# Stage boundaries of a two-block transformer kernel rebuilt: tile-wise norms, three products begun together, in-place weight slots, padded keys

## What is computed

```python
def first_block(x, ...):                    # two layers
    for l in range(2):
        u = rmsnorm(x, pre_mix_g[l])
        m = token_mixer(u, ...)              # 8 GQA heads (2 key heads) and 8 latent (MLA) heads, gates, w_o
        x = x + rmsnorm(m, post_mix_g[l])
        h = rmsnorm(x, pre_ffn_g[l]) @ w_ffn_up[l]          # 1024 -> 4096
        f = jnp.square(jax.nn.relu(h)) @ w_ffn_down[l]
        x = x + rmsnorm(f, post_ffn_g[l])
    return x

def second_block(x, ...):                   # layer 0: S5 scan, layer 1: stick-breaking attention
    h = rms_norm(x, norm_mix[0]);  x = x + s5_mixer(h, ...)
    x = x + conv_ffn(rms_norm(x, norm_ffn[0]), ...)          # 1024 -> 2 x 2816 -> 1024
    kv = rms_norm(x, norm_kv) @ kv_w
    h = rms_norm(x, norm_mix[1]);  x = x + stick_breaking_attention(h, w_q, k, v, w_o)
    x = x + conv_ffn(rms_norm(x, norm_ffn[1]), ...)
    return rms_norm(x, norm_final)
```

## Time and profile before

| | us |
|---|---|
| median of the runs | 3228.28 |
| the profiled execution | 3231.55 |
| its span | 3229.8 |
| TensorE matmul busy | 2923.6 (91%), 12788 matmuls |
| VectorE busy | 1589.4 (49%) |
| ScalarE busy | 1147.9 (36%) |
| GpSimd busy | 848.6 (26%) |
| granted TensorE clock, mean | 0.938 |
| weight chunk, from issue to landing, median | 3.4 |
| ScalarE: high half of a 1024-column chunk, of a 768-column chunk | 1.04, 0.84 |
| VectorE: low half of a 1024-column chunk, of a 768-column chunk | 1.23, 0.96 |
| ScalarE per norm tile: copy with gain, square | 0.71, 0.61 |

### The profile page before, as it was taken

One profiled execution on the slowest core, in us unless ns is written; L12 is line 12 of the kernel. 1 busy time (PEld: TensorE's weight loads), 2 busy tenths in 40 slices (PEclk: granted clock), 3 DMA queues, 4 the chain that ended last, 5 costly groups with the idle time before them and its releaser, 6 DMA issues.

```text
span 3229.8 us, 36156 instructions
## 1 busy us (share of the span) xinstructions
PE 2923.6 (91%) x12788; PEld 2341.5 (72%) x12788; DVE 1589.4 (49%) x2048; ACT 1147.9 (36%) x1716; POOL 848.6 (26%) x672
## 2 busy tenths in 40 slices
PE   7898997999979989979998674699999999999998
PEld 5566775888756667758886464578888778878887
DVE  4478434323264873343333767455542447655532
ACT  4355333223244552332223222233321336632322
POOL 2255003304132540132132837112210002212210
PEclk9799998999988999989999766799999998999999
DMA  3100231333220102212332110223333220023232
GB/s 127 33 27 27 87 95 62 97 98 98 92 66 27 33 27 93 96 62 96 98 98 79 52 34 16 69 78 98 98 98 106 89 82 4 27 85 96 94 104 85
DMA packets 75531, 236.91 MB, mean 73 GB/s; under 512 B 9520, under 2 KB 18144, under 8 KB 75360
## 3 DMA queue, kind: packets, MB, share of 16 engines
q1 hardware_dynamic: 74432, 231.43, 22.4%
q0 software_dynamic: 928, 3.21, 0.3%
HBM read 228.31 MB, written 2.10 MB: 71 GB/s over the span
## 4 chain that ended last, share of the span: by engine, by line
PE 62%; issue 22%; POOL 7%; DVE 6%; ACT 2%; SPq 1%; DMA 0%; POOLq 0%; DVEq 0%; ACTq 0%
PE bank L1615 20%; PE bank L1617 19%; PE bank L1616 19%; POOL TMP L732 3%; PE bank L1875 2%; POOL FF L717 1%; POOL FF L724 1%; DVE S5S L1489 1%; PE bank L1783 1%; DVE UL L1248 1%; POOL FF L737 1%; DVE S5M L1432 1%; PE bank L1830 1%; DVE S5S L1480 1%; SPq L665 1%
## 5 line engine op out<-in xcount | busy, mean ns | idle before, releaser
L1238 DVE TENSOR_TENSOR WL<-RAWW,WH 128x1024 fp32r<-128x1024 f32 (+2 forms) x424 | 538.5, 1270 | 1239.4 <-ACT WH L946 1239.0
L1615 PE MATMUL bank<-UH,WH 128*128 128x512 f32 (+1 forms) x1920 | 772.9, 403 | 151.0 <-DVE UL L1248 109.3
L1616 PE MATMUL bank<-UL,WH 128*128 128x512 f32 (+1 forms) x1920 | 761.3, 397 | 0.0
L1617 PE MATMUL bank<-UH,WL 128*128 128x512 f32 (+1 forms) x1920 | 760.3, 396 | 0.0
L946 ACT ACTIVATE WH<-RAWW 128x1024 fp32r<-128x1024 f32 (+2 forms) x424 | 437.7, 1033 | 846.0 <-PE bank L1617 839.1
L1615 PEld LDWEIGHTS bank<-UH,WH 128*128 128x128 f32 (+1 forms) x1920 | 368.3, 192 | 254.7 <-DVE UL L1248 96.8
L1616 PEld LDWEIGHTS bank<-UL,WH 128*128 128x128 f32 (+1 forms) x1920 | 369.4, 192 | 78.2 <-issue 2.5
L1617 PEld LDWEIGHTS bank<-UH,WL 128*128 128x128 f32 (+1 forms) x1920 | 368.4, 192 | 79.2
L698 POOL TENSOR_TENSOR SQUARES<-SQUARES,TMP 128x512 f32<-128x512 f32 x56 | 78.2, 1397 | 556.5 <-ACT TMP L966 554.8
L1615 PE MATMUL bank<-HH,WH 128*128 128x512 f32 x512 | 199.2, 389 | 0.0
L1616 PE MATMUL bank<-HL,WH 128*128 128x512 f32 x512 | 199.2, 389 | 0.0
(11 more groups left out here) (316 smaller groups left out, 4801.3 us busy)
## 6 DMA issues: line engine op xcount, KB each, us to landing
RAWW<-weights SPq DMA_DIRECT2D x424, 512.0 KB, 3.4
X<-x SPq DMA_DIRECT2D x8, 256.0 KB, 4.8
FF<-tables POOLq DMA_DIRECT2D x2, 1024.0 KB, 6.5
U<-S5U SPq DMA_DIRECT2D x16, 128.0 KB, 2.4
GEL<-U SPq DMA_DIRECT2D x128, 16.0 KB, 1.8
out<-FF SPq DMA_DIRECT2D x8, 256.0 KB, 2.5
S5B<-s_b POOLq DMA_DIRECT2D x1, 512.0 KB, 3.9
S5C<-s_c POOLq DMA_DIRECT2D x1, 512.0 KB, 4.5
```

The lines of the kernel that those rows point to most:

```text
L1238: dve.tensor_tensor(slot_words(WL, c % CUT, size), slot_words(RAWW, c % RAW, size), f32(slot_words(WH, c % CUT, size)), ALU.subtract).then ...
L1615: nc.tensor.matmul(out_, w[0], x_[0], start=start, stop=False, **how)
L1616: nc.tensor.matmul(out_, w[0], x_[1], start=False, stop=False, **how)
L1617: return nc.tensor.matmul(out_, w[1], x_[0], start=False, stop=stop, **how)
```

## The change

`SLOTS = 4`, `LEAD = 3` and `LINEAR_BANKS = (0, 1, 4, 5)` replace `RAW` and `CUT`. `WL` lies on top of `RAWW`: VectorE writes the low half over the raw chunk, both halves have four slots, and SyncE loads a slot when its product is through. Cuts are steps of their own. A linear run behind a norm issues its first three products k-tile by k-tile, side by side in three banks, then a tree of sums on VectorE over the eight squares (now in FF), then the fourth product, then one ones-matmul for the factor; evacuations catch up by two per product. The next norm's work follows each finished tile of X. VectorE scales all eight post-norm tiles. The keys of the two key heads lie in separate tiles, padded with zeros to 128 rows. The layer loop is written out twice. Constants come on ScalarE's queue, X and the first weights in turn on SyncE's.

```diff
+    def product(x):
+        ring = LEAD + 1 if norm and x >= 2 else 2
...
+        mm[x].bank = LINEAR_BANKS[mm[x].j % (LEAD + 1)] if norm else mm[x].j % 2
+    if norm:
+        for x in range(LEAD):
+            product(x)
+        for step in mm:
+            step.lead = mm[:]
+        if early:
+            early()
+        plan.add("tree", norm=norm)
+    for x in range(len(mm), len(jobs) + 1):
         if x < len(jobs):
+            product(x)
+            plan.cut_to(done_of(mm[x]) + 1)
+        elif ahead:
+            plan.cut_to(plan.total["c"] + LEAD - (2 if ahead == "post" else 1))
+        if norm and x == LEAD:
+            plan.add("stat", "g tot", norm=norm)
+            if late:
+                late()
+        while evacuated < min(x, 1 + 2 * (x - LEAD) if norm else x):
+            after["evac"](evacuated, mm[evacuated])
+            evacuated += 1
+    if ahead:
+        plan.cut_to(plan.total["c"] + LEAD - 1)
...
+def into_x(plan, norm, kind="evac_res"):
+    def evac(m, mm):
+        plan.add(kind, "x", m=m, j=mm.j, bank=mm.bank, done=done_of(mm))
+        plan.add("norm_tile", k=m, norm=norm)
+    return evac
...
+    def early():
+        plan.add("s5_params0")
+        plan.add("s5_params1")
     def ssm_input(x, mm):
-        if x < 4:
-            plan.add(f"s5_params{x}")
-        if x == 2:
+        if x == 0:
+            plan.add("s5_params3")
             plan.add("s5_b")
-        if 3 <= x <= 5:
-            plan.add("s5_power", p=x - 2)
-        if 4 <= x <= 5:
-            plan.add("s5_c", half=x - 4)
-        if x >= 6:
-            plan.add(f"s5_grid{x - 6}")
+        if 2 <= x <= 4:
+            plan.add("s5_power", p=x - 1)
+        if x in (2, 4):
+            plan.add("s5_c", half=(x - 2) // 2)
+        if x in (5, 6):
+            plan.add(f"s5_grid{x - 5}")
+    linear(plan, [dict(tile, rhs="u")] * DT,
+           dict(norm=norm, early=early, late=lambda: plan.add("s5_params2"), evac=ssm_input))
...
-        RAWW = at("RAWW", 18, [P, RAW, SLOT])
-        WH = at("WH", 34, [P, CUT, SLOT], F32R)
-        WL = at("WL", 42, [P, CUT, SLOT], F32R)
+        RAWW = at("RAWW", 18, [P, SLOTS, SLOT])
+        WL = at("WL", 18, [P, SLOTS, SLOT], F32R)
+        WH = at("WH", 34, [P, SLOTS, SLOT], F32R)
-        KH = at("KH", A0 + 16, [P, SEQ], F32R)
+        KH = at("KH", A0 + 68, [P, KV_HEADS, SEQ], F32R)
...
-                        sp.wait_ge(lo.sem, it * RAW + (k + 1))
+                        sp.wait_ge(used.sem, it * SLOTS + (k + 1))
...
 # GpSimd, once per layer, behind the first sum of the layer
+                pool.wait_ge(total.sem, total.after(l, 0))
                 pool.dma_start(FF[:, 0:4, :], tables.rearrange("k p n -> p k n")).then_inc(tab_in, 16)
+                for v in (KH, KL):
+                    ins = pool.memset(f32(v[:]), 0.0)
...
 # ScalarE
+            def norm_tile(l, norm, k, gain):
+                act.wait_ge(x_done.sem, x_done.room(l, DT * norm.version + k))
+                if gain is not None:
+                    act.activation(UH[:, k, :], X[:, k, :], ACT.Copy, scale=gain[:, k:k + 1]).then_inc(uh.sem, 1)
+                act.activation(FF[:, k, :], X[:, k, :], ACT.Square).then_inc(squared.sem, 1)
...
 # VectorE
+            def add_tree(l, norm):
+                dve.wait_ge(squared.sem, squared.after(l, norm.v + DT - 1))
+                for n in range(3):
+                    w = DT >> n + 1
+                    a, b = (FF[:, DT - 2 * w + k * w:DT - w + k * w, :].rearrange("p k n -> p (k n)") for k in range(2))
+                    if n:
+                        dve.wait_ge(tree.sem, tree.after(l, norm.t + n - 1))
+                    dve.tensor_tensor(b, b, a, ALU.add).then_inc(tree.sem, 1)
...
                 elif kind == "post":
-                    for k in range(DT + 1):
-                        if k < SCALED:
+                    for k in range(DT + 2):
+                        if k < DT:
                             dve.tensor_tensor(FF[:, k, :], FF[:, k, :], RCQ[:], ALU.mult).then_inc(scaled.sem, 1)
+                        if 1 <= k <= DT:
                             t = k - 1
...
+                        if k >= 2:
+                            tile_rest(to, norm.n, k - 2, gain)
...
 # TensorE
+            def lead_jobs(l, jobs, ready):
+                for st in jobs:
+                    pe.wait_ge(bank_free.sem, bank_free.room(l, st.j) - (2 if st.ring > 2 else 0))
+                for k in range(DT):
+                    pe.wait_ge(*ready(k))
+                    for st in jobs:
+                        if k == 0:
+                            pe.wait_ge(lo.sem, lo.after(l, st.c))
+                        cols = slice(k * st.cols, (k + 1) * st.cols)
+                        ins = product(BANK[st.bank][0:st.cols, :], (WH[:, st.c % SLOTS, cols], WL[:, st.c % SLOTS, cols]),
+                                      (UH[:, k, :], UL[:, k, :]), k == 0, k == DT - 1)
...
-                        rows, i = slice(st.h // QT * HD, st.h // QT * HD + HD), st.h % QT
-                        qs = QH[rows, i, q], QL[rows, i, q]
-                        ks = KH[rows, :], KL[rows, :]
+                        qs = QH[:, st.h % QT, q], QL[:, st.h % QT, q]
+                        ks = KH[:, st.h // QT, :], KL[:, st.h // QT, :]
...
-            with pe.Fori(0, LAYERS) as l:
+            for l in range(LAYERS):
```

More of the change, by code:

```diff
@@ L212, in first_products @@
         group = {"q": 1 + i, "k": 1 + QT, "cq": 2 + QT, "ckv": 3 + QT}.get(what)
-        ev[x] = plan.add("evac_" + what, take, i=i, x=x, j=mm.j, done=mm.c, group=group)
+        ev[x] = plan.add("evac_" + what, take, i=i, x=x, j=mm.j, bank=mm.bank, done=mm.c, group=group)
         if x >= 2:
@@ L288, in hidden @@
         else:
[L289 to L293 removed]
+            plan.add("evac_cup", "cu", m=x // 2, j=mm.j, bank=mm.bank, done=mm.c)
+    linear(plan, [dict(kt=[DT], cols=P, rhs="u")] * (2 * C_TILES), dict(norm=norm, evac=hidden))
@@ L372, in plan_second @@
             plan.add("sb_out", "o", h=x - 3)
-    linear(plan, [dict(tile, rhs="y2")] * DT,
-           dict(evac=lambda x, mm: plan.add("evac_res", "x", m=x, j=mm.j, done=mm.c)))
-    conv_ffn_steps(plan, 1, 3)
-    plan.add("final", "f a:4 s:3 g", version=4)
+    norm = plan.add("norm", NORM, gain=("ffn", 1), version=3)
+    linear(plan, [dict(tile, rhs="y2")] * DT, dict(ahead="res", evac=into_x(plan, norm)))
+    norm = conv_ffn_steps(plan, 1, norm, dict(version=4))
+    plan.add("tree", norm=norm)
+    plan.add("stat", "g tot", norm=norm)
+    plan.add("final")
     return plan
@@ L1219, in _ @@
             act.sem_inc(expd.sem, 2)
-            cut(0, 0, SLOT)
-            with act.Fori(0, LAYERS) as l:
+            act.wait_ge(mats_cut, 1)
+            for k in range(DT):
+                norm_tile(0, LAYER.steps[0], k, LP[:, 0, 0:DT])
+                if k < LEAD:
+                    cut(0, k, SLOT)
+            for l in range(LAYERS):
                 for st in LAYER.steps:
@@ L1396, in second @@
                 kind = st.kind
-                if kind == "mm":
-                    cut_next(2, st, SECOND_WORDS)
-                elif kind in ("norm", "regain"):
+                if kind == "cut":
+                    cut(2, st.c, SECOND_WORDS[st.c])
+                elif kind == "regain":
                     g = S_GAIN[st.gain]
                     gained_rest(2, st, SP_[:, g:g + DT])
+                elif kind == "norm_tile" and st.norm.gain:
+                    g = S_GAIN[st.norm.gain]
+                    for k in range(st.k - 1, st.k + (st.k == DT - 1)):
+                        if k >= 0:
+                            tile_rest(2, st.norm.n, k, SP_[:, g:g + DT])
+                elif kind == "tree":
+                    add_tree(2, st.norm)
                 elif kind == "stat":
```

403 lines of the change are left out of this document (195 added, 208 removed).

## The result

The changed kernel takes 3166.7 us (median of 4, 3159.5 to 3172.6) where the one before takes 3225.3: ratio 0.9817, 95% interval 0.9802 to 0.9833. The medians are 58.6 us apart. The profiled executions went from 3231.55 to 3166.94, 64.6 us (the one before lies 6 us above its median, so part of this is chance); the prediction had 78.7. The direction and most of the mechanisms hold, and the terms are off by 14 us on balance.

A forecast was written before the change was run, and what follows sets the result against it. TensorE, busy 91%, was taken to wait longest for low halves UL at 20 stage boundaries with a norm. Terms 26.6+9+2.6+18-3.5-11+32+5 = 78.7 us off 3231.55 give 3152.9, 3151 for runs; range 3110 to 3198.

The forecast's parts named there:

- Padded keys: First eight heads: full rows save 19 us of gaps and 19 of low clock; 32 of 38 taken.
- The first rival: First eight heads: padding moves nothing, clock and gaps come from elsewhere; 3183 us, chance 0.15.
- FFN entries: Post-norm boundary before each layer's FFN: four products done at Z+35.3 (Z: last product's end), 13.3 us gained twice, 26.6.
- S5 entry: Entry of the second block: parameter steps ahead of the fourth weight cut delay the S5 response; 11 us lost.
- Second block: Its norm boundaries: 7.4 at the first FFN, 6.6 behind w_o, 4 before keys and values; 18 us gained together.
- fifth product at Z+26.6 ... four would be done at Z+34: gain 7.4: First FFN of the second block, timed from Z, the last product's end: 7.4 us gained over the kernel before.
- Cuts wait no longer for the product two back: Weight slots: evacuations stand free of the cuts; 2.6 us per layer in the gate stage, 5 in both.
- Layer to layer and start: q stages between the layers and at the start: 9 and 2.6 us gained.
- two loop passes of 8.3 and 7.7 ... give Z+62.4: q stage between layers: seventh product starts 62.4 us after the last product's end, before at Z+71.8; gain 9.
- Gate stage: TensorE's waits of 2.6 us per layer for weight cuts go; 5 us gained in both layers.
- End: Kernel end: tree on the path, first output op at Z+8.4 (Z: last product's end) against Z+4.9; 3.5 us lost.
- Slower: Rival: clock stays low through the first eight heads in both layers; 100 us lost against 47 won, 3281, chance 0.06.

The follow-up runs named there:

- e1: Changed kernel with the first eight heads' score products reading only their group's 64 rows again: 3194.2 us, ratio 0.9917.
- e2: Changed kernel with only the middle of each score product's three matmuls reading 64 rows in the first eight heads: 3184.0 us, ratio 0.9883.
- e11: Kernel before with the padded keys alone added (score products of 128 rows): 3194.7 us, ratio 0.9913.
- e4: Changed kernel with the second S5 parameter step, an exponential on ScalarE, queued behind the norm's factor: 3155.9 us, ratio 0.9798.
- e7: Changed kernel with GpSimd's 16 wide S5 operations held until VectorE's three power steps are done: 3150.0 us, ratio 0.9774.
- e5: Changed kernel with weights cut one product further ahead from the fifth product on, in stages that begin three together: 3156.6 us, ratio 0.9798.
- e8: Changed kernel beginning two output tiles together instead of three at each norm, with only two weights cut ahead: 3155.3 us, ratio 0.9797.
- e12: e10 with two output tiles instead of three begun together in the q stages and three second-block entries: 3112.0 us, ratio 0.9657.
- e10: Changed kernel with e4, e5, e7, each begun product waiting for its own bank, and last squares added as they come: 3123.2 us, ratio 0.9695.

## Why the prediction was right, and where its sizes were off

- **Padded keys**, 29.8 for 32: right, and both causes are real, with e1, e2 and e11 behind it. Their sizes were less exact: the gaps are some 13 us for 19, because 0.3 us per unit was counted for units that wait for other things too, and the clock some 17 of the 19. The first rival is excluded. The rule of the Trainium skill that a single K=32 matmul takes the time of K=128 (TensorE: Matmul & The Clock Gate, "Why this matters for your kernels") can't be carried over to a stream that changes between 64 and 128 rows: there each change costs 0.1 or 0.2 us. The other rule of the Trainium skill, that transposes don't count for the clock (same page, Part 4: PE-mode transpose), no run here shows to hold anything down: with four transposes of ten instructions the clock was 1.00.
- **FFN entries**, 26.2 for 26.6: right at each step.
- **S5 entry**, -10.9 for -11: right in sum and in cause (e4). What I had not seen is that the power steps behind it are slow for another reason, which cost more than the order (e7).
- **Second block**, 9.7 for 18: the step "fifth product at Z+26.6 ... four would be done at Z+34: gain 7.4" was right up to the fifth product and stopped there. The evacuations that had been put off come behind it, and with them waits of 1.5 and 2.1 us for WL in both conv FFNs, 7.2 of the missing 8.3 us. "Cuts wait no longer for the product two back" looked at slots; the cuts wait in the queues of ScalarE and VectorE, behind the convolution steps. e5 shows the half of it that order can mend.
- **Layer to layer and start**, 3.1 for 11.6 together: the step "two loop passes of 8.3 and 7.7 ... give Z+62.4" failed. The seventh product starts at Z+65.3 between the layers, past the bound of 64 that I had named, and at 72.8 at the start, where 68.1 was forecast. Each q stage is then longer: 107.0 us from its first product to the scores, with 100.5 before. Three outputs finished at once are three chains of evacuation, square, turn and rest one behind another, and TensorE waits 6.1 us in the middle. With two tiles the longest such wait is 2.7 to 3.0 us (e8, e12). In e12 both q stages take 101; in e8, where the third weight is cut late behind a post-norm, only the first is shorter (99.5) and the second takes 106.1, and the cuts ahead alone (e5) change nothing in the second (106.9).
- **Gate stage**, 11.2 for 5 with the latent heads (-0.2): I took the eight waits of the earlier trace rows at their 2.6 us. A wait of 0.35 us in the list was a gap of 0.51 from start to start, and the matmul behind it let the next start 0.1 late. From one stop to the next it took 16.97 us and takes 16.32, so eight stops are some 5 us a layer. The stage went from 137.3 to 132.3 and 131.0; the last 1.3 are its first product, which takes 7.2 us with the clock at 0.50 in part of it and 5.8 at 1.00, and falls either way whatever the edit. The mechanism was right, a term mis-sized: a stop costs more than the wait that the list shows.
- **End**, -4.5 for -3.5: the tree, and its ones-matmuls at the lower clock (2.04 us for the pair).

The misses of opposite sign (+6.2 in the gate stage, -8.3 in the second block, -8.5 in layer to layer and start, -2.2 in the heads) cancel in part; that the sum was closer than its parts is luck. Not settled is why the first q stage and the latent heads with the gate stage trade 2.5 to 3 us between builds that don't touch them; half of it is the clock in the gate stage's first product.

Two figures of the prediction are wrong as sums. The forecast for the runs should read 3149.6 (3228.3 less 78.7), not 3151. And the rival "Slower" set 230 us of heads at half clock against "some 130" now: 130 is the warm pace, and the heads took 173.8 (90.3 and 83.5). So 56 us would have been lost and not 100, against 47 won: some 3237 and not 3281, at the edge of what tells from no change. The clock left 0.50 early in both layers, so it didn't come up.

## What to carry to other kernels

Work that is begun early is evacuated late and in a bunch: price the stage until the bunch is worked off, with every queue that it passes, and not only until TensorE starts again. How many outputs to begin before a factor depends on what their evacuations start: where each starts a chain across engines, as in the q stage, two were better than three by 6 to 9 us, of which 2.6 came back in the next stage (e12 against e10). Where the tiles are there already it made 1.4 us in three entries, once the cuts stood further ahead. With two, keep the third product's weights cut ahead of the norm's sum (e12 against e8). Before moving work to a second engine, look whether the same instruction has two durations in the trace; where it has, order is worth more than balance.

## What the hardware showed that I had not expected

- VectorE and GpSimd beside each other don't share the loss evenly. VectorE's operations of 512 columns on two SBUF operands went from 0.7 to 2.4 us and more, about one of GpSimd's 1024-column operations each, while GpSimd's went from 2.0 and 2.4 to 2.35 and 2.67. Operations of VectorE with one SBUF operand were slowed too: 0.55 to 2.70 for 768 columns (e7).
- With three of ten matmuls at 64 rows the clock stayed at 0.50 through a stretch of 15 us in which TensorE was busy 15.00 us, and rose 41.0 and 24 us behind the first score of the layers. With one of ten it rose after 16.5 and 14 us, with full rows after 10 and 11.
- A change from 128 to 64 rows costs 0.1 us in a stream, and back 0.2.
- A wait of 0.35 us on TensorE in the profile is a gap of 0.51 us from start to start.
